# Moving the attention, the merge and the output projection of chunk 0 into earlier stages of a decoder-layer kernel

## The reference

```
h = RMSNorm(x); z = h @ W_in  ->  q, k, v | x_rnn, y_rnn | g_attn, g_rnn
A: attention, 8 heads of 64; q and k normalised; T5 relative bias;
   per query its own block of 256 keys (causal) and the 3 past blocks
   with the largest q . mean(k)
B: conv1d of 4 on x_rnn, then the gated linear recurrence h_t = a_t h_(t-1) + b_t,
   a and b from two block-diagonal products; times GeLU(y_rnn)
x = x + W_out( sigmoid(g_attn) * (A @ P_attn) + sigmoid(g_rnn) * (B @ P_rnn) )
x = x + W_2( relu(RMSNorm(x) @ W_1)^2 )
```

## Time and profile before

| | |
|---|---|
| median of 3 runs | 2372.44 us (2369.84 to 2372.55) |
| the profiled execution | 2370.91 us |
| its span on the slowest core, core 7 | 2369.0 us (cores: 2356.4 to 2369.0) |
| TensorE (PE) busy | 2261.0 us, 95% |
| ScalarE (ACT), VectorE (DVE), GpSimd (POOL) busy | 1329.1, 1170.3, 606.6 us |
| mean granted clock of PE, core 7 | 0.980 |
| moved by DMA | 373.44 MB, mean 158 GB/s |

### The profile page before, as it was taken

The page is one execution under the profiler, slowest core; times in us unless marked ns, Lnnn a source line. Parts: engine busy times, 40 slices in busy tenths (PEclk is TensorE's granted clock), DMA queues, the critical chain, the costliest instruction groups (busy, mean ns, idle before and its releaser), DMA issues.

```text
span 2369.0 us, 43806 instructions; the slowest of 8 cores (2356.4 to 2369.0 us)
## 1 busy us (share of the span) xinstructions
PE 2261.0 (95%) x14494; PEld 1103.7 (47%) x14494; DVE 1170.3 (49%) x2225; ACT 1329.1 (56%) x2343; POOL 606.6 (26%) x593
## 2 busy tenths in 40 slices
PE   4999799999999968999999999999999999999999
PEld 2445334444444434454555555554555455554444
DVE  3777577778778754544444333324232432332332
ACT  3665586776767735464647547564765475563111
POOL 4677444344344310201102001101101100111200
PEclk9999899999999986999999999999999999999999
DMA  7967715456461448356646556557455654653543
GB/s 175 268 204 196 146 53 121 120 116 143 125 143 60 147 125 229 103 162 184 176 146 192 178 166 193 147 160 225 124 170 169 190 153 146 181 162 142 167 171 125
DMA packets 194598, 373.44 MB, mean 158 GB/s; under 512 B 15507, under 2 KB 106684, under 8 KB 176316
## 3 DMA queue, kind: packets, MB, share of 16 engines
q1 hardware_dynamic: 188684, 336.04, 45.4%
q0 software_dynamic: 5696, 34.61, 8.9%
HBM read 332.30 MB, written 91.76 MB: 179 GB/s over the span
## 4 chain that ended last, share of the span: by engine, by line
PE 86%; issue 4%; DMA 3%; DVE 3%; POOL 2%; ACT 1%; SPq 0%; DVEq 0%; ACTq 0%; POOLq 0%
PE bank L479 86%; DMA s_xs<-x 1%; POOL s_ssq L479 1%; DMA q_s<-s_qst 1%; DMA s_t1r<-t_s 1%; DVE s_cv L479 1%; DMA s_wy<-wr_p 0%; ACT s_PT L479 0%; DVE s_ii L479 0%; DVE s_mT L479 0%; DMA s_qT<-s_mskT 0%; DVE s_t1r L479 0%; DVE s_ktm L479 0%; DVE s_ssq L479 0%; POOL s_rr L479 0%
## 5 line engine op out<-in xcount | busy, mean ns | idle before, releaser
L479 ACT ACTIVATE s_PT<-bank 128x512 bf16<-128x512 f32 (+3 forms) x1152 | 590.4, 562 | 312.7 <-PE bank L479 193.7
L479 PE MATMUL bank<-s_uT,s_wsl 128*128 128x512 bf16 x2048 | 518.9, 379 | 0.0
L479 PE MATMUL bank<-s_h2T,s_wsl 128*128 128x512 bf16 x2048 | 516.8, 380 | 0.8 <-DVE s_h2T L479 0.8
L479 PEld LDWEIGHTS bank<-s_Vr,s_PT 128*128 128x128 bf16 x4224 | 274.5, 99 | 268.0 <-issue 32.4
L479 PE MATMUL bank<-s_qT,s_kTr 80*128 80x512 bf16 (+3 forms) x1152 | 377.7, 372 | 7.5 <-ACT s_PT L479 4.2
L479 PE MATMUL bank<-s_Vr,s_PT 128*128 128x65 bf16 x4224 | 316.6, 195 | 11.3 <-ACT s_PT L479 11.0
L479 ACT ACTIVATE s_rl<-bank 128x512 f32<-128x512 f32 x256 | 152.9, 598 | 302.8 <-PE bank L479 292.7
L479 PEld LDWEIGHTS bank<-s_h2T,s_wsl 128*128 128x128 bf16 x2048 | 190.9, 98 | 180.6 <-issue 3.1
L479 PEld LDWEIGHTS bank<-s_uT,s_wsl 128*128 128x128 bf16 x2048 | 184.9, 98 | 162.4 <-issue 3.1
L479 DVE TENSOR_TENSOR s_uT<-s_rl 128x512 bf16<-128x512 f32 x176 | 122.1, 694 | 267.1 <-ACT s_rl L479 266.9
L479 DVE TENSOR_TENSOR s_x1T<-bank,s_x1T 128x512 f32<-128x512 f32 x128 | 88.2, 691 | 311.7 <-PE bank L479 311.0
(11 more groups left out here) (119 smaller groups left out, 2733.7 us busy)
## 6 DMA issues: line engine op xcount, KB each, us to landing
s_wsl<-wff_s SPq DMA_DIRECT2D x128, 1024.0 KB, 5.8
s_xs<-x SPq DMA_DIRECT2D x32, 512.0 KB, 7.3
wff_s<-wff_p POOLq DMA_DIRECT2D x16, 1024.0 KB, 11.3
s_rmr<-rm_s SPq DMA_DIRECT2D x64, 256.0 KB, 4.6
s_t1r<-t_s SPq DMA_DIRECT2D x64, 256.0 KB, 4.4
s_x1T<-xT SPq DMA_DIRECT2D x64, 256.0 KB, 5.0
outT<-s_x1T SPq DMA_DIRECT2D x64, 256.0 KB, 5.7
h_s<-s_hT SPq DMA_DIRECT2D x32, 256.0 KB, 3.7
```

The costliest lines, as they stand in the source:

```text
L479: return P.add(eng, lambda e, m=meth, kw=kw: getattr(e, m)(**kw), reads, writes, cost=c_, lat=lat, fam=fam, tag=tag or (writes[0] if write ...
```

## The change

- **Attention of chunk 0** becomes units of its own (attention0), put into the q,k,v stage, two for each token tile from tile 10 on and four from tile 24 on. q, k and v of chunk 0 stay in SBUF (qc0, kc0, vc0); q of chunk 0 is no longer stored. It uses bank 6 for S and bank 5 for AV, has no mask rows, and stores its result to oT_s. The bias table is made at token tiles 5, 7 and 9.
- **Its merge**: GA of chunk 0 multiplies its attention with wpa, which is loaded in four parts on POOL's queue (WPS), before it stores t1; GR of chunk 0 loads that, adds it on POOL and stores mT of chunk 0 to mT_s.
- **Its output projection** is listed right behind the last stageB, ahead of GR of the last chunk; mT is loaded in early.
- Chunk 1's attention has no mask either; masks are made from chunk 2 on, with gate matmuls from block 4 on.
- SBUF of the attention stage is laid out anew. wo and mT lie over wx and wy, x1T 0 to 7 over xr, qT of chunk 1 over cv, h2T over a chunk of hT, the first two weight slabs over wga, uT over the first two tiles of wgr and wpr.
- GR's projection matmuls wait each for its own orn tile, not for all eight.
- At the start the second and third q,k,v weight are loaded after x tiles 1 and 2 have landed.
- **Fill-in matmuls** (keep_busy): where the planner's model shows PE idle for over 700 ns, matmuls of ones into the bank whose last readers finish first are added, for 80% of the gap.

```
-    def emit(self, nc, final_keys):
+    WGAP = 700.0
+    def keep_busy(self, order, deps, filler):
...
+            t = self.t0[i]
+            a = max(end, filler[1]) + 200.0
+            if t - a > self.WGAP - 200.0:
...
+                a = max(a, fin + self.HOPT)
+                m = int((t - a) * 0.8 / 216.0)
+                for q in range(m):
+                    j = self.add("tensor", lambda e, b=b: filler[0](e, b), cost=216.0, lat=170.0, tag="fill")
+                    deps.append(set(rd) | set(filler[2]))
...
+    def emit(self, nc, final_keys, filler=None):
...
-            dma("gpsimd", wqkv[j], wqkv_d[j].rearrange("p (a b) -> p a b", a=8), "wqkv%d" % j, [], ["wqkv%d" % j])
-        for t in range(1, NXS):
-            load_x(t)
+            dma("gpsimd", wqkv[j], wqkv_d[j].rearrange("p (a b) -> p a b", a=8), "wqkv%d" % j, [], ["wqkv%d" % j], extra=P.after("xs%d" % j) if j else ())
+            if j == 0:
+                for t in range(1, NXS):
+                    load_x(t)
...
+        def attention0():
...
+                    op("tensor", "matmul", ["kc0:%d" % kt] + ["qc0:%d" % i for i in range(kt, 4)], ["B6"], tag="S0", out=bankf[6][:, 0:nq],
+                       lhsT=kc0[r0:r0 + 64, hp, q0:q0 + 128], rhs=qc0[r0:r0 + 64, hp, q0:CH], start=True, stop=True)
+                    op("vector", "tensor_tensor", ["B6", "BT"], ["B6"], tag="bias0", ...)
+                    op("scalar", "activation", ["B6"], ["PTa%d" % pi], out=PTa[pi][:, 0:nq], in_=bankf[6][:, 0:nq], func=AF.Exp, fam="expln")
+                    for qt in range(kt, 4):
+                        op("tensor", "matmul", ["PTa%d" % pi, "vc0"], ["B5"], tag="AV0", ...)
...
-            if t == 8:
+            if t == 5:
                 bias_table(P.after("hT%d" % (t % NHT)))
-            if t == 14:
+            if t == 7:
                 bias_table1()
+            if t == 9:
+                for g in range(4):
+                    bias_table2(g)
+                at0 = attention0()
+            if t >= 10:
+                for _ in range(2 if t < 24 else 4):
+                    if at0:
+                        at0.pop(0)()
...
+            if c == 0:
+                b = bank()
+                for kt in range(4):
+                    op("tensor", "matmul", ["oTb", "wps%d" % (p % 2)], ["B%d" % b], tag="pa", ...)
+                op("vector", "scalar_tensor_tensor", ["B%d" % b, "t1_%d" % s], ["t1_%d" % s], ...)
+                if m % 2 == 1 and p < 2:
+                    WPS(p + 2)
...
-                op("tensor", "matmul", ["orn%d" % i for i in sos] + ["wpr%d" % p], ...)
+                op("tensor", "matmul", ["orn%d" % sos[kt], "wpr%d" % p], ...)
...
+            if c == 0:
+                dma("sync", t1x[s], t1_s[0, m], "t1x%d" % s, ["t1_s0_%d" % m], ["t1x%d" % s])
+                op("gpsimd", "tensor_tensor", ["t2_%d" % s, "t1x%d" % s], ["mst%d" % s], out=mst[s], in0=t2[s], in1=t1x[s], op=ALU.add)
+                dma("sync", mT_s[:, m, :], mst[s], "mst%d" % s, ["mst%d" % s], ["mT_s%d" % m])
+                return
...
         stageB(NCH - 1, 1, early)
+        for _, f in outproj(0):
+            f()
+        at1.pop(0)[1]()
+        first.append(kv1(1, 0))
...
-        g0 = gating(0)
...
-        extend(outproj(0))
-        dense.append((6000.0, lambda: None))
...
-            goal = tot0 * (i + 1) / 6 if i < 5 else tot0 + (tot - tot0) * min(1.0, (dcum[i] - dcum[4]) / ((last - dcum[4]) * 0.98))
+            goal = tot * min(1.0, dcum[i] / (last * 0.98))
...
+        def fill(e, b):
+            return e.matmul(out=bankf[b], lhsT=ones, rhs=ones.unsqueeze(1).to_broadcast([128, 4, 128]), start=True, stop=True)
```

More of the change, by code:

```diff
@@ L582, in bias_table3 @@
[L582 to L586, removed]
+            b = tbank()
+            op("tensor", "matmul", ["tabx", "Gs"], ["B%d" % b], out=bankf[b][0:8, 0:384], lhsT=tabx[0:33, :], rhs=Gs[0:33, :], start=True, stop=True)
@@ L793, in build_nc @@
         t2 = [alloc("t2_%d" % i, [CH], F32) for i in range(2)]
[L794 to L795 removed]
+        t1x = [alloc("t1x%d" % i, [CH], F32) for i in range(2)]
+        mst = [alloc("mst%d" % i, [CH], BF16) for i in range(2)]
         pB_peak = cur[0]
@@ new lines, in build_nc @@
+        wpa = alloc("wpa", [4, D], BF16)
+        alloc("gap2", [(endR + 16384 - cur[0]) // 2], BF16)
+        PT += [alloc("PT%d" % i, [CH], BF16) for i in (4, 5)]
+        oT = [None, alloc("oT1", [4, CH], BF16)]
+        NRL = 2
+        rl = [alloc("rl0", [CH], F32)]
+        assert cur[0] == baseC, (cur[0], baseC)
+        h2T = alloc("h2T", [8, CH], BF16)
+        NW = 4
+        wsl = [alloc("wsl%d" % i, [4096], BF16) for i in range(2)]
+        uT = alloc("uT", [16, CH], BF16)
+        wsl += [alloc("wsl%d" % i, [4096], BF16) for i in (2, 3)]
@@ L1054, in attention @@
             units.append((0.0, lambda: QLOAD(c)))
-            units += [(100.0, lambda tl=tl: GM(c, tl)) for tl in range(TPC)]
+            if c > 1:
+                units += [(100.0, lambda tl=tl: GM(c, tl)) for tl in range(TPC)]
             for h in range(NH):
@@ L1238, in build_nc @@
                 extend(w2)
-        queue = [(u[0], u[1], 0) for u in at0[5:]]
-        tot0 = sum(q_[0] for q_ in queue)
-        for c in range(1, NCH):
-            us = attention(c)
-            if c == 1:
-                queue[16:16] = [(u[0], u[1], 0) for u in us[:5]]
-                us = us[5:]
-            for u in us:
+        queue = [(u[0], u[1], 1) for u in at1]
+        for c in range(2, NCH):
+            for u in attention(c):
                 queue.append((u[0], u[1], c))
@@ L1263, in build_nc @@
                 dense[i][1]()
-        P.emit(nc, ["out%d_%d" % (c, dt_) for c in range(NCH) for dt_ in range(8)])
+        ones = onesf.bitcast(BF16)[:, 0:128]
+        def fill(e, b):
+            return e.matmul(out=bankf[b], lhsT=ones, rhs=ones.unsqueeze(1).to_broadcast([128, 4, 128]), start=True, stop=True)
+        P.emit(nc, ["out%d_%d" % (c, dt_) for c in range(NCH) for dt_ in range(8)], (fill, P.latest["onesf"]))
         st.pop().close() if len(st) > 1 else None
```

283 lines of the change are left out of this document (189 added, 94 removed).

## The result

**The changed kernel takes 2317.12 us (median of 3 executions; 2316.98 us the fastest) against 2371.14 us before: a ratio of 0.9774 [0.9754, 0.9793] with its 95% interval, 54 us less.** Now and then an execution of any of these kernels is slower as a whole, with a lower granted clock on the cores of one die; times and ratios here leave such executions out. The forecast was 2311 us with 2282 to 2348 us as its range. The profiled execution took 2318.37 us; its span is 2316.8 us on core 5 (cores 2306.9 to 2316.8 us), and PE is busy for 2270.7 us of it, 98%.

What follows compares the result with a forecast made beforehand. PE was taken as the bound nearly everywhere, with loss left in four places. Terms -65 (change of stages), +15 (q,k,v stage), 0 (merge), -10 (start) and 0 (fill-ins) sum to -60: 2370.9 to 2311 us, range 2282 to 2348 us.

Steps and rivals of the forecast that it cites:

- The change of stages: Change to the attention stage, 810 to 965 us: loss of 60 us shrinks to 10, 15 us of PE work leaves; -65 us.
- the sum of 33 us idle and some 27 us of slow clock: 810 to 965 us: PE's idle time plus slow granted clock, taken as 60 us of loss.
- The q,k,v stage, +15: Chunk 0's attention moved into the q,k,v stage adds 7.6 us of PE work and 7 us of waits; +8 to +40.
- The slower rival: PE waits for each exp of chunk 0's 32 units in the q,k,v stage: 83 us in place of 7, 2387 us; 9%.
- Merge in the gate stage, 0: Chunk 0's gate stage: 6.9 us of added matmuls hidden by 18.4 us idle; 0, from -15 to +15 us.
- POOL's wait at the wpr issue still there: Sign for chunk 0's gate stage: POOL's 14.8 us wait of a wpr load for a late q store remains.
- The 13% rival: Chunk 0 of the gate stage loses its POOL wait of 14.8 us: 2296 us; 13%.
- The start, -10: Second and third q,k,v weights wait for token tiles 1 and 2, so PE starts earlier; -10 us, from 0 to -15.
- The mark (before 27 us): Sign for the start: the first long run of q,k,v matmuls begins before 27 us.
- Fill-ins, 0: Matmuls of ones in PE's foreseen gaps: 0; at most 86 us of cost or about 27 us of clock loss regained.
- The first rival, half a repair: Change of stages only half repaired, PE still idles before chunk 7's projection: about 27 us of gain lost, 2338 us; 20%.
- The bounds: The forecast's own bounds, 10 us each way on -65, +15 and the start, said to reach from 2285 to 2335 us.

Runs made afterwards that it cites:

- with 80 rows: The changed kernel with chunk 1's S matmuls reading 80 rows again: 2307.09 us, 0.9703 of the kernel before; run once more, 0.9718.

## Why the prediction was right, point by point

- **The change of stages, -50 for the loss and -15 for the work moved: the mechanism was right, one price was left out.** The signs named came: chunk 0's exps lie from 130.9 to 218.6 us, PE is idle for 3.35 us from 810 to 965 us (below 10 was named) at a clock of 1.00, and chunk 7's projection begins at 852.46 us right behind the 64 matmuls of the output projection. It gave -54.1 us, -57.4 us in the median. The step that failed is the price of S for chunk 1: the forecast took "0.216" for a matmul of 512 columns and put the vanished mask down as "under 1 us" of gain. Without its mask rows, S has 64 rows and costs 0.2 us more; 64 of them are 13 us, and -54.1 - 13 = -67 us (-70 us in the median) would be beside the -65. What was wrong as a reason is the sum of 33 us idle and some 27 us of slow clock: in the kernel before with fill-ins the clock alone gives at most 4 us of them. The gain reached its size without it: leaving the attention and merge out gave 53.7 us, and the rest is the projection and what no run prices.
- **The q,k,v stage, +15: +16.1 us by the marks, for other reasons in part.** The term was 8 us of work and 7 us of new waits. Between the two marks, before and after (columns of the earlier trace rows), PE's idle time is 9.1 us both times:

```profile
34.91:254.03 219.12, 210.01 (x1306) 106.54 (x1307) 158.18 (x248) 137.78 (x225) 159.08 (x203) 1.00 0.75 206
...
26.64:261.86 235.22, 226.11 (x1453) 115.46 (x1454) 176.12 (x305) 149.80 (x257) 164.82 (x206) 1.00 0.76 201
```

So no wait grew in total, and all 16.1 us are busy time: beside the 7.6 us of work, the 64 rows of its 32 S matmuls (32 x 0.2 = 6.4 us) and 22 matmuls of ones (4.8 us), less 2.7 us of smaller pieces. That these came near the 7 us for waits is luck. The slower rival, a wait for each exp, is refuted by 2.3 us of waits for exps in the whole run.
- **Merge in the gate stage, 0: -5.9 us between the two cores shown, -0.2 us in the median, as a sum of two parts.** The sign "POOL's wait at the wpr issue still there" came out otherwise, and it rested on a row of core 7. On core 3 that wait is as long, on core 0 it is 5.7 us; on the other five cores POOL waits at that issue for DVE, 4.5 to 7.6 us. In the kernel before, the lines of core 3 and of core 1 are:

```profile
POOL s_wpr L484 <- DMA q_s<-s_qst: 15.4, 1, 15.4
...
POOL s_wpr L484 <- DVE s_cv L479: 4.7, 1, 4.7
```

After, the waits of POOL from 235 to 345 us, here on core 5, are for PE on all eight cores:

```profile
POOL s_wps L535 <- PE bank L530: 5.1, 2, 4.7
POOL s_wpr L535 <- PE bank L530: 4.7, 1, 4.7
```

The 13% rival's price, 14.8 us, was thus that of two cores in eight, and even there some 8 us: from the last q,k,v run to the 64th matmul with wga it is 51 to 52 us on the cores 3 and 7 and 42 to 45 us on the others. After, it is 47 to 52 us on every core, 5 us more in the median. So on most cores the idle time hid only a part of the merge's 6.9 us. The other 5 us came off later, between the 128th and the 192nd matmul with wga (78.6 to 73.8 us, medians), where the last part of the bias table, at 397 us on core 7, had stood; it is now made at 124 to 127 us. That the two parts cancel is luck. Why no wait for the q store is left at that issue wasn't tried.
- **The start, -10: -8.3 us at the first run, 4.0 us in the whole by the ratios.** The mark (before 27 us) was met at 26.64. The rule of the Trainium skill, "DMA: Bandwidth & Descriptors", section "Issuing engines are not separate DMA queues", would have given 0 by equal sharing. The trace agrees with the sharing: the tokens land earlier and the last weight later (37.9 us and not 32.4 us as in the kernel before). The first long run could still begin 8.3 us earlier, since it works on token tile 1, which lands at 17.4 us and not at 24.3 us. The time lies between the rule's 0 and the term's -10, and by the ratios the run can't tell 4 us from 0.
- **Fill-ins, 0:** shown, within 3 to 5 us, by the run without them.
- **The first rival, half a repair,** did not come: no wait for s_orn stands before chunk 7's projection. It shows where the parts are taken away: 10.1 us idle from 810 to 965 us with the output projection in its old place, 20.0 us in the kernel before without chunk 0's attention.
- **The bounds:** 10 us each way for three terms reach from 2281 to 2341 us, not from 2285 to 2335 us as the forecast says. The result lies inside either.

## What to carry to other kernels

Work that runs almost alone on its chains can cost several times its PE time (53.7 us for some 15 us of matmuls here), and the gain of moving it is that loss, less what it costs in the new place. Before an operand is made narrower, look at the distance between starts of its neighbours: fewer rows can cost more than they save, and busy time hides it. A low clock beside idle time is not a second loss until a run that lifts it alone has shown a gain. And a wait read on the slowest core may be that core's own: read the other cores before it goes into a sum.

## What the runs showed of the hardware

**A change between 64 and 128 rows costs PE some 0.1 us; one between 80 and 128 rows costs nothing that shows.** The weight loads (PEld, start and length) of the changed kernel, and behind them those with 80 rows, show how:

```profile
906.36 0.09 PEld L530 LDWEIGHTS bank<-s_qT,s_kTr 64*128 64x128 bf16 x1
906.68 0.10 PEld L530 LDWEIGHTS bank<-s_h2T,s_wsl 128*128 128x128 bf16 x1 [0.23 <-issue]
...
910.66 0.10 PEld L530 LDWEIGHTS bank<-s_qT,s_kTr 80*128 80x128 bf16 x1
910.69 0.10 PEld L530 LDWEIGHTS bank<-s_h2T,s_wsl 128*128 128x128 bf16 x1
```

The first two start together with their own matmul (906.36 and 906.68 us above). With 80 rows the load for W1 starts at 910.69 us, 0.22 us before its matmul at 910.91 us, and lies under the S matmul. So at each change between 64 and 128 rows the load isn't hidden, at some 0.1 us each, two for each S. Added up over the 64 S matmuls of chunk 1 in the trace, the steps around them are some 12 us longer than with 80 rows. Where two 64-row matmuls follow each other, PE shows that the change is dear and not the 64 rows:

```profile
854.28 0.60 PE L530 MATMUL bank<-s_qT,s_kTr 64*128 64x512 bf16 x2
854.82 0.61 PE L530 MATMUL bank<-s_hTb,s_wgr 128*128 128x512 bf16 x2
```

From the first of the two to the next matmul it is 0.54 us: 0.22 us for the first and 0.32 us for the second, which stands before the change. Were each 64-row matmul dear, it would be 0.64 us. The Trainium skill, "TensorE: Matmul & The Clock Gate", Part 3, "What overlaps and what doesn't", says that a weight load overlaps with matmuls in flight only when its row group differs. The traces don't fit that: loads over all 128 rows hide under 128- and 80-row matmuls, at 0.216 us a step, and those at a change to or from 64 rows don't, and the measurement decides. Which other counts of rows are dear, and why, was not tried.

**The granted clock can be lifted without a gain that shows:** 0.81 to 0.96 and 0.76 to 0.84 with the time at 0.999 [0.9979, 1.0002].
